# Expert weights in three ring places of 4 MB in place of six of 2 MB

## The reference

```
gate, idx = lax.top_k(jnp.swapaxes(aff, 1, 2), cap)       # 16 experts, cap = 32 tokens each
xs = jax.vmap(lambda hb, ib: hb[ib])(h, idx)              # (16, 32, 1024)
a = jnp.einsum('becd,edf->becf', xs, w_gate)              # w_gate (16, 1024, 2048)
u = jnp.einsum('becd,edf->becf', xs, w_up)                # w_up   (16, 1024, 2048)
y = jnp.einsum('becf,efd->becd', jax.nn.silu(a) * u, w_down) * gate[..., None]   # w_down (16, 2048, 1024)
```

## Time and profile before

| | |
|---|---|
| median of 3 runs | 1908.63 us |
| the profiled execution | 1907.21 us |
| its span, from the first to the last instruction | 1905.4 us |
| outside the span | 1.81 us |
| mean granted TensorE clock | 0.855 of full speed |
| PE busy | 1457.4 us (76%) |
| DMA queue of SP | 523.08 MB, 67.8% of 16 engines' span |
| the experts' loop | about 960 to 1894 us of the span |

### The profile page before, as it was taken

How to read it: one execution, slowest core, us unless ns; L and a number is a source line. 1 busy time by engine, 2 the same in 40 slices (tenths; PEclk the granted TensorE clock), 3 DMA queues, 4 the chain that set the end, 5 groups by cost and what they waited for, 6 DMA issues and landing times.

```text
span 1905.4 us, 22301 instructions
## 1 busy us (share of the span) xinstructions
PE 1457.4 (76%) x9153; PEld 932.9 (49%) x9153; DVE 541.6 (28%) x936; ACT 497.2 (26%) x715; POOL 395.4 (21%) x168
## 2 busy tenths in 40 slices
PE   6799878769899797998877766676766677667674
PEld 5678767659799795787622221122221222212221
DVE  5843467762544505166410000000000000000001
ACT  4353566643556434254300000000000000000001
POOL 3433322316577563442000000000000000000000
PEclk8899899879899898999888878778787877887887
DMA  7634332414354333232359999999999999999995
GB/s 263 231 133 177 135 131 103 163 45 133 119 181 154 122 122 133 88 133 89 133 246 428 429 428 429 428 429 429 429 428 428 429 428 429 429 429 428 429 428 253
DMA packets 101120, 524.02 MB, mean 275 GB/s; under 512 B 7961, under 2 KB 30897, under 8 KB 76353
## 3 DMA queue, kind: packets, MB, share of 16 engines
q1 hardware_dynamic: 100841, 523.08, 67.8%
q10 hardware_dynamic: 216, 0.06, 0.0%
HBM read 522.07 MB, written 1.05 MB: 275 GB/s over the span
## 4 chain that ended last, share of the span: by engine, by line
DMA 44%; PE 34%; DVE 14%; ACT 5%; issue 2%; POOL 1%; SPq 0%; DVEq 0%; ACTq 0%; PEldq 0%
DMA ring<-in_w_down 22%; DMA ring<-in_w_up 21%; PE ps L559 7%; PE ps L563 6%; PE ps L560 6%; PE ps L982 3%; PE ps L996 2%; DVE arena L1408 2%; PE ps L915 1%; PE ps L546 1%; PE ps L606 1%; DVE arena L1542 1%; ACT ring_r L1027 1%; DVE arena L1573 1%; DVE bc L1347 1%
## 5 line engine op out<-in xcount | busy, mean ns | idle before, releaser
L1335 POOL TENSOR_TENSOR ring_r<-ring,ring_r 128x1024 fp32r<-128x1024 f32 (+1 forms) x164 | 395.2, 2421 | 485.8 <-ACT ring_r L1027 485.5
L559 PE MATMUL ps<-arena_r,ring_r 128*128 128x272 f32 (+2 forms) x1296 | 409.2, 316 | 53.6 <-POOL ring_r L1335 19.3
L982 PE MATMUL ps<-ring,arena 128*32 128x512 f32 x2048 | 312.0, 760 | 132.4 <-DMA ring<-in_w_up 116.4
L563 PE MATMUL ps<-arena_r,ring_r 128*128 128x272 f32 (+2 forms) x1296 | 392.6, 303 | 0.0
L559 PEld LDWEIGHTS ps<-arena_r,ring_r 128*128 128x128 f32 x1296 | 258.5, 199 | 69.7 <-issue 43.4
L996 PE MATMUL ps<-ring,arena 128*32 128x512 f32 x1024 | 178.6, 832 | 108.1 <-DMA ring<-in_w_down 101.2
L563 PEld LDWEIGHTS ps<-arena_r,ring_r 128*128 128x128 f32 x1296 | 258.6, 200 | 2.8
L982 PEld LDWEIGHTS ps<-ring,arena 128*32 128x32 f32 x2048 | 68.8, 130 | 359.0 <-DMA ring<-in_w_up 180.6
L560 PE MATMUL ps<-uT_r,ring_r 128*128 128x272 f32 x768 | 230.1, 300 | 0.0
L1027 ACT ACTIVATE ring_r<-ring 128x1024 fp32r<-128x1024 f32 (+1 forms) x164 | 169.9, 1043 | 36.7 <-PE ps L560 17.0
L560 PE MATMUL ps<-arena_r,ring_r 128*128 128x272 f32 (+2 forms) x528 | 162.9, 309 | 0.0
(11 more groups left out here) (328 smaller groups left out, 1382.2 us busy)
## 6 DMA issues: line engine op xcount, KB each, us to landing
ring<-in_w_gate SPq DMA_DIRECT2D x64, 2048.0 KB, 26.0
ring<-in_w_up SPq DMA_DIRECT2D x64, 2048.0 KB, 19.6
ring<-in_w_down SPq DMA_DIRECT2D x64, 2048.0 KB, 25.7
ring<-in_w_in SPq DMA_DIRECT2D x20, 2048.0 KB, 11.2
ring<-in_w_ada SPq DMA_DIRECT2D x12, 2048.0 KB, 8.1
ring<-in_ffn_w_up SPq DMA_DIRECT2D x22, 1024.0 KB, 6.5
ring<-in_w_out SPq DMA_DIRECT2D x6, 2048.0 KB, 9.0
ring<-in_ffn_w_down SPq DMA_DIRECT2D x4, 2048.0 KB, 8.5
```

Of the source, the lines that this page charges most:

```text
L559: pe.matmul(o, hi[:, k, :], r_(xhi(k0 + k)), start=first and k == 0, stop=False)
L563: mm = pe.matmul(o, lo[:, k, :], r_(xhi(k0 + k)), start=False, stop=last and k == nk - 1)
L982: mm = pe.matmul(ps[32 * j:32 * j + 32, half, :], xs[:, kt, :], w[:, k, 512 * j:512 * j + 512], start=kt == 0, stop=kt == KT - 1)
L1335: pool.tensor_tensor(r_(w), w, f_(rounded(c)), ALU.subtract).then_inc(ev("w_lo"), 1)
```

## The change

Units of the experts become twice as large (4 MB) and the ring has three places of 4 MB, each made of two neighbouring old places: the same 12 MB of SBUF. Each expert has 6 units (G0, G1, U0, U1, D0, D1 in the text) instead of 12. For w_gate and w_up, k becomes 4: a partition holds four neighbouring rows of 8 KB, 32 KB in one piece. For w_down a DMA fetches two of the old units, so each partition has two pieces of 16 KB that lie 2 MB apart in HBM. `units_used` rises once for each 4 MB, and all who wait on it count in sixes. The gather's step over the tokens goes from 2 to 4.

```
-            return tokens.rearrange("t (b p k) -> t b k p", p=P, k=2)[:, kt // 2, kt % 2, :]
+            return tokens.rearrange("t (b p k) -> t b k p", p=P, k=4)[:, kt // 4, kt % 4, :]
...
-                s = i % RING
-                if i < 8:
-                    w = a["w_gate_2" if i < 4 else "w_up_2"][0, after:][e]
-                    src = w.rearrange("(b p k) c -> b p k c", p=P, k=2)[i % 4]
-                    dst = ring[:, s, :].rearrange("p (k c) -> p k c", k=2)
+                s = i % BIG
+                dst = ring[:, 2 * s:2 * s + 2, :]
+                if i < 4:
+                    w = a["w_gate_2" if i < 2 else "w_up_2"][0, after:][e]
+                    src = w.rearrange("(b p k) c -> b p k c", p=P, k=4)[i % 2]
+                    dst = dst.rearrange("p a (k c) -> p (a k) c", k=2)
                 else:
                     w = a["w_down_2"][0].rearrange("e f c -> (e f) c")[bass.ds(e * DE, DE), :]
-                    src = w.rearrange("(b p j) c -> b p j c", p=P, j=4)[i - 8]
-                    dst = ring[:, s, :].rearrange("p (j c) -> p j c", j=4)
+                    src = w.rearrange("(b p j) c -> p b (j c)", p=P, j=4)[:, 2 * (i - 4):2 * (i - 4) + 2]
                 sp.wait_ge(ev("units_used"), used)
-                sp.dma_start(dst, src).then_inc(ev(f"slot{s}_loaded"), 16)
+                sp.dma_start(dst, src).then_inc(ev(f"big{s}_loaded"), 16)
-            for i in range(RING):
-                before = [u for u in range(U0) if u % RING1 == i]
-                expert_unit(before[-1] + 1 if before else u_in2[-1] + 1, 0, i)
+            for i in range(BIG):
+                before = [u for u in range(U0) if u % RING1 in (2 * i, 2 * i + 1)]
+                expert_unit(before[-1] + 1, 0, i)
             with sp.Fori(0, NE - 1) as e:
-                for i in range(RING, 12 + RING):
+                for i in range(BIG, 6 + BIG):
-                    expert_unit(e * 12 + (U0 + i - RING + 1), e, i % 12, i // 12)
+                    expert_unit(e * 6 + (U0 + i - BIG + 1), e, i % 6, i // 6)
...
                 for half in range(2):
-                    for i in range(4):
-                        s = (4 * half + i) % RING
-                        pe.wait_ge(ev(f"slot{s}_loaded"), e * 32 + (slot_count[s] + 16 * (1 + (4 * half + i) // RING)))
-                        w = ring[:, s, :].rearrange("p (k c) -> p k c", k=2)
-                        for k in range(2):
+                    for i in range(2):
+                        u = 2 * half + i
+                        s = u % BIG
+                        pe.wait_ge(ev(f"big{s}_loaded"), e * 32 + 16 * (1 + u // BIG))
+                        w = ring[:, 2 * s:2 * s + 2, :].rearrange("p a (k c) -> p (a k) c", k=2)
+                        for k in range(4):
                             for j in range(4):
-                                kt = 2 * i + k
+                                kt = 4 * i + k
...
                 for i in range(4):
+                    u = 4 + i // 2
+                    s = u % BIG
+                    if i % 2 == 0:
+                        pe.wait_ge(ev(f"big{s}_loaded"), e * 32 + 16 * (1 + u // BIG))
...
-                    mm.then_inc(ev("units_used"), 1)
+                    if i % 2 == 1:
+                        mm.then_inc(ev("units_used"), 1)
```

More of the change, by code:

```diff
@@ L39 @@
 RING1 = 5
+BIG = 3
 HB = 4
@@ L490, in expert_unit @@
             def expert_unit(used, e, i, after=0):
-                s = i % RING
-                if i < 8:
-                    w = a["w_gate_2" if i < 4 else "w_up_2"][0, after:][e]
-                    src = w.rearrange("(b p k) c -> b p k c", p=P, k=2)[i % 4]
-                    dst = ring[:, s, :].rearrange("p (k c) -> p k c", k=2)
+                s = i % BIG
[4 more added lines that the diff above has]
+                    dst = dst.rearrange("p a (k c) -> p (a k) c", k=2)
                 else:
                     w = a["w_down_2"][0].rearrange("e f c -> (e f) c")[bass.ds(e * DE, DE), :]
-                    src = w.rearrange("(b p j) c -> b p j c", p=P, j=4)[i - 8]
-                    dst = ring[:, s, :].rearrange("p (j c) -> p j c", j=4)
+                    src = w.rearrange("(b p j) c -> p b (j c)", p=P, j=4)[:, 2 * (i - 4):2 * (i - 4) + 2]
                 sp.wait_ge(ev("units_used"), used)
-                sp.dma_start(dst, src).then_inc(ev(f"slot{s}_loaded"), 16)
-            for i in range(RING):
-                before = [u for u in range(U0) if u % RING1 == i]
-                expert_unit(before[-1] + 1 if before else u_in2[-1] + 1, 0, i)
+                sp.dma_start(dst, src).then_inc(ev(f"big{s}_loaded"), 16)
+            for i in range(BIG):
+                before = [u for u in range(U0) if u % RING1 in (2 * i, 2 * i + 1)]
+                expert_unit(before[-1] + 1, 0, i)
             with sp.Fori(0, NE - 1) as e:
-                for i in range(RING, 12 + RING):
-                    expert_unit(e * 12 + (U0 + i - RING + 1), e, i % 12, i // 12)
-            for i in range(RING, 12):
-                expert_unit((NE - 1) * 12 + (U0 + i - RING + 1), NE - 1, i)
+                for i in range(BIG, 6 + BIG):
+                    expert_unit(e * 6 + (U0 + i - BIG + 1), e, i % 6, i // 6)
+            for i in range(BIG, 6):
+                expert_unit((NE - 1) * 6 + (U0 + i - BIG + 1), NE - 1, i)
             for w in range(2):
@@ L990, in _ @@
                 for i in range(4):
-                    s = (8 + i) % RING
-                    pe.wait_ge(ev(f"slot{s}_loaded"), e * 32 + (slot_count[s] + 16 * (1 + (8 + i) // RING)))
-                    w = ring[:, s, :].rearrange("p (j c) -> p j c", j=4)
+                    u = 4 + i // 2
+                    s = u % BIG
+                    if i % 2 == 0:
+                        pe.wait_ge(ev(f"big{s}_loaded"), e * 32 + 16 * (1 + u // BIG))
+                    w = ring[:, 2 * s + i % 2, :].rearrange("p (j c) -> p j c", j=4)
                     for half in range(2):
@@ L1312, in _ @@
             with act.Fori(0, NE) as e:
-                act.wait_ge(ev("units_used"), e * 12 + (U0 + 4))
+                act.wait_ge(ev("units_used"), e * 6 + (U0 + 2))
                 act.activation(sa, ps[:, 0, :], ACT.Silu).then_inc(ev("gate_silu"), 1)
@@ L1316, in _ @@
                 act.activation(heT[:], ps[:, 2, :].rearrange("p (b c) -> p b c", b=4), ACT.Copy).then_inc(ev("heT_ready"), 1)
-                act.wait_ge(ev("units_used"), e * 12 + (U0 + 12))
+                act.wait_ge(ev("units_used"), e * 6 + (U0 + 6))
                 act.activation(ye[:, 0:512], ps[:, 0, :], ACT.Copy).then_inc(ev("y_half"), 1)
@@ L1907, in _ @@
                 dve.wait_ge(ev("gate_silu"), e + 1)
-                dve.wait_ge(ev("units_used"), e * 12 + (U0 + 8))
+                dve.wait_ge(ev("units_used"), e * 6 + (U0 + 4))
                 tt(he, sa, ps[:, 1, :], ALU.mult).then_inc(ev("hidden"), 1)
-                dve.wait_ge(ev("units_used"), e * 12 + (U0 + 12))
+                dve.wait_ge(ev("units_used"), e * 6 + (U0 + 6))
                 dve.tensor_copy(ye[:, 512:1024], ps[:, 1, :]).then_inc(ev("y_other"), 1)
```

## The result

The changed kernel takes 1922.49 us in the median (1920.23 to 1924.73, 4 runs) against 1908.77 us before (4 runs); the ratio is 1.0071 (95% interval 1.0053 to 1.0088), 13.7 us slower, where 2.2 us faster was forecast and 1912.5 us was the range's end. The profiled execution has a span of 1920.2 us, 14.8 us more than before.

What follows compares the result with a forecast made beforehand. The experts were taken to run against the DMA engines (share 1.00 at 428 GB/s). Start +1.71, end +1.9, packets -4.9 and fewer DMAs -0.9 gave -2.2 us: median 1906.4 us, range 1902.5 to 1912.5 us.

Steps and rivals of the forecast that it cites:

- I charge nothing; a tenth more would be +0.6 us once: Gather matmuls reading tokens with step 4 instead of 2: no cost, judged by hidden transposes; later experts covered by margin.
- The margin is 6 us, or 5: Head of each expert: G0 used 21.7 to 23.4 us after D1's landing, queue holds 29.4 us, so no pause: 0.
- The queue runs dry after the gather (slower): Rival at the head of experts: low clock lengthens PE's path, loads pause; at 0.6 us each +6.8, 1915.4 us; chance 0.07.
- Start: Start of the stream: first DMA of the loop waits until g1 is used, with nothing in the queue; +1.71 us.
- Packets: w_gate and w_up loads: 8 packets per engine instead of 16, 10 ns saved for each; -4.9 us (0 to -7.0).
- little or no shorter pace: Rival on w_gate and w_up loads: longer packets save little or nothing; 1911.3 us, or 1909.6 us; chance 0.17.
- Fewer DMAs: Expert stream: 186 DMAs become 93, each saving a small semaphore packet per engine at 10 ns; -0.9 us (0 to -1.3).
- 12,000 fewer packets: Sign expected in the changed kernel's whole trace: 12,000 fewer packets, some over 16 KB.
- End: After the last landing PE has a 4 MB unit to work off instead of one old unit; +1.9 us (up to 3.6).
- The layout in HBM reads slower: Rival on the expert loads: runs farther apart in HBM read slower; one per cent of stream 9 us, 1915.5 us; chance 0.09.

Runs made afterwards that it cites:

- the last experiment: Kernel before plus nine groups of 8 extra matmuls or transposes behind each expert's gather, weights read with various steps; transposes with step 4 about 0.12 us per record.
- the kernel without a step: Changed kernel (32 KB runs, three places), but ScalarE writes tokens in the gather's order so it reads without a step: 1906.50 us, ratio 0.9990.
- the old layout in three places: Changed kernel's three places of 4 MB, but w_gate and w_up in 16 KB runs and a gather step of 2: 1912.40 us, ratio 1.0020.

## Why the prediction was wrong

*"I charge nothing; a tenth more would be +0.6 us once"*, for the gather's step, is the step that failed. The gather took 7.67 us in every expert, +3.7 us where it had run at the full clock (3.95 us, nine of 16) and +1.3 to +2.2 us in the others, and it was not covered by the margin. The row I rested on, L987, was the wrong neighbour: it does read with a step of 4, but it is a transpose, and the last experiment shows transposes with that step at 0.12 us per record while the plain matmuls of the gather take 0.24. The trace of before had the gather itself only with a step of 2. A cost that no row shows should have been bounded by a factor, not by a tenth.

A page of the Trainium skill would have warned ("Advanced Engine Details and Errata", section "Memory Cachelines"): SBUF has lines of 16 bytes, and two accesses in a line are needed for full speed. Steps of 1 and 2 floats make four and two accesses in a line, 3.75 and 3.95 us; a step of 4 makes one, 7.67 us. The gather's rows agree, those of the transposes don't.

*"The margin is 6 us, or 5"* was too large by 2.8 us. I counted the queue's 29.4 us from the landing, but the landing is seen after the last data of the slowest engine; by then the others are in the next load. The kernel before shows it: 186 units of 4.894 us from 972.6 us end at 1882.9, and the landing is at 1885.70. Windows of the kernel before, ahead of that landing:

```profile
1882.00:1883.00 1.00, 0.80 (x8) 0.00 (x0) 0.00 (x0) 0.00 (x0) 0.00 (x0) 1.00 1.08 459
1883.00:1884.00 1.00, 0.00 (x0) 0.00 (x0) 0.00 (x0) 0.00 (x0) 0.00 (x0) 1.00 0.35 148
1884.00:1885.00 1.00, 0.00 (x0) 0.00 (x0) 0.00 (x0) 0.00 (x0) 0.00 (x0) 1.00 0.08 33
```

The share falls to 0.35 and 0.08 in the last 3 us ahead of the landing. 29.4 - 2.8 = 26.6 us for the new load's first data, 25.7 for its issue; the changed kernel puts the limit between 26.3 us (no pause) and 26.9 us (a pause), so this is good to about 1 us. With both terms the trace of before would have shown the danger: 21.7 to 23.4 us and 3.7 to 2.0 more for the gather come to 25.4, right at the limit. It would not have given the size of the loss: the passages came out at up to 27.6 us. With the gather of before G0 was used after 22.8 us, and nothing paused.

*"The queue runs dry after the gather (slower)"* was the right rival, with its place and mechanism, at a chance of 0.07 and for the wrong reason: I let only the clock lengthen the path. Its price was short as well: 923.4 - 909.5 = 13.9 us of stream were lost beside the kernel without a step, and a pause is followed by reading below pace, which I hadn't priced. Summed over 1 us windows from the first D1 to the last, the engines' busy time is 3.8 us longer than without a step and their idle time 10.1 us longer, so about 10 us are silence and 4 slow reading.

*Start:* forecast +1.71, measured +3.66: 1.28 us of the difference are the first gather (7.67 for 6.39), 1.06 that G0 took 6.48 us from take-up to issue instead of 5.42, and -0.39 that the gather began earlier in this execution. *Packets:* forecast -4.9, measured -4.5 over the 15 experts from D1 to D1 (58.73 to 58.43 us each); the rival "little or no shorter pace" is refuted, and so are the 3.6 ns per packet worked out from the 3 cycles of the Trainium skill ("DMA: Bandwidth & Descriptors", section "Why small descriptors are slow (HBM only)"): 4.5 us over 60 x 8 packets saved is 9.4 ns, where 10 was forecast. *Fewer DMAs:* forecast -0.9, measured nothing (58.73 us in six places and in three). The forecast's 12,000 fewer packets were miscounted: its own terms give 64 x 128 + 96 x 16 = 9,728, as measured. *End:* forecast +1.9, measured +1.8 (5.34 us for x32 against 3.56 for x16). *"The layout in HBM reads slower"* is refuted: 431 GB/s with 32 KB runs, and the old layout in three places, in which every load has two pieces 2 MB apart, runs at 428.

So the packets' and the end's terms were right, and with the gather's cost out of the way the sum came out near: the kernel without a step measured -1.9 us against before, -2.2 forecast. Part of that is luck. The profiled executions of the two differ by only -0.6 us: start +2.4, stream -4.7, end +1.7.

## What to carry to other kernels

When a layout changes to please the DMA, look at every engine that reads through it: ask what the step does to the weight loads, and bound it by a factor, not by a tenth. When a ring gets coarser, work out the longest time from a landing to the release, subtract the spread of the engines and the issue latency from what the queue holds, and compare the two; a cost that six places hide can be the whole result with three. The remedy is often cheap: permuting during a copy that happens anyway, or a finer wait on the last load, took back 16 and 12 us here.

## What the hardware showed that I had not expected

- The gather's matmuls, with fp32 weights of 128 x 128 read by a step of 16 bytes, took 0.240 us per record at a granted clock of 1.00 and of 0.50 alike. With 8 bytes it was 0.123 us at 1.00, with 4 bytes 0.117 us at 1.00 and 0.204 us at 0.50. A transpose with 16 bytes took 0.12 us at 1.00.
- A queue that has run empty starts below its pace. In the changed kernel, at the first load of the loop and after a pause:

```profile
976.00:980.00 4.00, 4.00 (x40) 1.11 (x36) 0.00 (x0) 0.60 (x1) 0.00 (x0) 1.00 1.08 393
```

  At a share of 1.08 that is 364 GB/s per full occupation against 431 in the steady stretch.
- One packet of 32 KB exists and saves 9.4 ns against two of 16 KB (58.43 for 58.73 us per expert), at 431 instead of 428 GB/s.
- The landing of a load says when its slowest engine is done. In the changed kernel it came 0.8 to 2.2 us late in five passages in which the 16 engines together were hardly idle.
